# Sample attention of a hybrid encoder layer: keys turned by VectorE in 32x32 squares, FoX scores as plain fp32 products, only the wanted output blocks turned

## The reference, cut to what matters

```
# FoX branch, 8 heads x 64: 512 cached keys and the 16 new ones
s = q @ k_all.T / 8 + c[q] - c[k]      (masked where k > q)
o_fox = softmax(s) @ v_all
# memory branch, 4 heads x 128: 256 cached keys
o_mem = softmax(qm @ mk.T / sqrt(128)) @ mv
```

## Time and profile before

| | before |
|---|---|
| timed runs | 1926.58 to 1926.63 us, median 1926.61 |
| span of the profiled execution | 1926.4 us |
| PE busy | 1903.4 us, 99% |
| DVE, ACT, POOL busy | 1222.8, 842.7, 516.6 us |
| DMA, mean | 105 GB/s |
| FoX samples on PE | about 545 to 668 us |
| memory samples on PE | about 780 to 864 us |

### The profile page before, as it was taken

The page is one execution under the profiler, slowest core; times in us unless marked ns, Lnnn a source line. Parts: engine busy times, 40 slices in busy tenths (PEclk is TensorE's granted clock), DMA queues, the critical chain, the costliest instruction groups (busy, mean ns, idle before and its releaser), DMA issues. The chain is left out here.

```text
span 1926.4 us, 33099 instructions
## 1 busy us (share of the span) xinstructions
PE 1903.4 (99%) x12655; PEld 1869.4 (97%) x12655; DVE 1222.8 (63%) x2293; ACT 842.7 (44%) x1672; POOL 516.6 (27%) x547
## 2 busy tenths in 40 slices
PE   9999999999999999999999999999999999999998
PEld 8999999999999999999999999999999999999997
DVE  6685545454557666554334467687777977777765
ACT  7454434353546544443223332344444544444445
POOL 1004324250612123000000004276544433333320
PEclk9999999999999999999999999999999999999999
DMA  6451312213266643444233222233333433333323
GB/s 197 114 134 50 94 47 66 83 35 94 55 231 206 203 137 99 146 154 131 64 104 93 70 88 72 94 100 91 122 89 92 123 91 88 88 88 88 89 93 99
DMA packets 243601, 202.40 MB, mean 105 GB/s; under 512 B 16750, under 2 KB 217966, under 8 KB 243317
## 3 DMA queue, kind: packets, MB, share of 16 engines
q1 hardware_dynamic: 243445, 200.29, 34.8%
HBM read 166.62 MB, written 33.64 MB: 104 GB/s over the span
## 5 line engine op out<-in xcount | busy, mean ns | idle before, releaser
L1654 PE MATMUL ps<-act_hi,w_hi 128*128 128x384 f32 x1128 | 386.9, 343 | 0.9 <-DVE w_lo L597 0.6
L1654 PE MATMUL ps<-act_hi,w_lo 128*128 128x384 f32 x1128 | 378.0, 335 | 0.0
L1654 PE MATMUL ps<-act_lo,w_hi 128*128 128x384 f32 x1128 | 377.6, 335 | 0.0
L597 DVE TENSOR_TENSOR w_lo<-w_raw,w_hi 128x512 fp32r<-128x512 f32 (+1 forms) x200 | 198.0, 990 | 122.3 <-ACT w_hi L579 121.7
L1638 PE MATMUL ps<-ffs_hi,w_hi 128*128 128x288 f32 x832 | 245.8, 295 | 1.0 <-DVE h L2646 0.6
L1638 PE MATMUL ps<-ffs_hi,w_lo 128*128 128x288 f32 x832 | 245.2, 295 | 0.0
L1638 PE MATMUL ps<-ffs_lo,w_hi 128*128 128x288 f32 x832 | 244.9, 294 | 0.0
L1623 PE MATMUL ps<-bp_hi,pw_hi 128*128 128x288 f32 x784 | 231.6, 295 | 0.2 <-DVE pw_lo L2601 0.2
L1623 PE MATMUL ps<-bp_lo,pw_hi 128*128 128x288 f32 x784 | 231.3, 295 | 0.0
L1623 PE MATMUL ps<-bp_hi,pw_lo 128*128 128x288 f32 x784 | 231.2, 295 | 0.0
L579 ACT ACTIVATE w_hi<-w_raw 128x512 fp32r<-128x512 f32 (+1 forms) x200 | 152.6, 763 | 164.5 <-PE ps L1638 119.4
(11 more groups left out here) (356 smaller groups left out, 4190.7 us busy)
## 6 DMA issues: line engine op xcount, KB each, us to landing
w_raw<-in_w_down_dram SPq DMA_DIRECT2D x112, 256.0 KB, 3.4
pair_raw<-in_w_up_dram SPq DMA_DIRECT2D x28, 1024.0 KB, 5.5
w_raw<-in_w_in_dram SPq DMA_DIRECT2D x44, 512.0 KB, 4.4
merged<-prod SPq DMA_DIRECT2D x48, 192.0 KB, 2.0
prev<-merged SPq DMA_DIRECT2D x48, 192.0 KB, 3.8
foxs_vraw<-in_cache_fox_v_dram SPq DMA_DIRECT2D x8, 1024.0 KB, 6.1
foxs_kraw<-in_cache_fox_k_dram SPq DMA_DIRECT2D x7, 1024.0 KB, 5.6
x_in<-in_x_prompt_dram SPq DMA_DIRECT2D x8, 512.0 KB, 4.5
```

The source lines that it names most:

```text
L597: nc.vector.tensor_tensor(W[c % 2][1][:, 0:kt, :], w_raw[c % 2][:, 0:kt, :], W[c % 2][0][:, 0:kt, :].bitcast(F32), ALU.subtract).then_inc( ...
L1654: last = nc.tensor.matmul(bank(b)[:, 0:width], W[k][a][:, t, :], moving[z][:, t, j * width:(j + 1) * width], start=(t == 0 and n == 0), st ...
```

## The change

- Keys are loaded in another layout: four DMAs for each sample, one for each quarter y of the partitions, with rows of 512 bytes. Partition 32y + r gets tokens r, 32 + r and so on, and of them the 128 channels of group y.
- `turn_keys` is gone from PE. DVE turns the keys with its own transpose, which turns each 32x32 square in its place (`keys_turned`, four instructions a sample). Because of the new layout the squares make whole rows of keys, but the channels of a group now lie in another order (32 channels of each of four groups), and the queries (`qs_raw`, `mqs_raw`) are laid out in the same way. A mask `own_head`, made once by POOL, multiplies the queries so that other heads' rows are zero.
- FoX scores take the turned keys and the queries as they are, as plain fp32: 8 products of 128x264 in place of 24 fp32r ones, and no split. `kt` and `qpad` have two homes each, used in turn. Memory keys are turned into `kt_raw` and then split by ACT and DVE as before, from SBUF.
- The values' result is read by ACT (not DVE) in four small copies, of each head's rows only the columns wanted (`own_values`), into an `om` of 128x128. One transpose turns it. `out_sum` of FoX has four small additions in place of two.
- In the projection of q and k, ACT copies the sample tokens in four quarters in place of one, and DVE's rest of them is gone (8 blocks each).

```diff
+        qs_raw = tensor("qs_raw", [P, BT, P], R3_AT + 7168)
+        ks_raw = tensor("ks_raw", [P, BT, P], R3_AT + 11264)
...
+        sf = dict(kraw=tensor("foxs_kraw", [P, PAST // QUAD, P], R_AT), kt=[tensor(f"foxs_kt{k}", [P, 4, ST * P + NQ], R_AT + 8192 + 16 * (ST * P + NQ) * k) for k in range(2)],
+                  qpad=[tensor(f"foxs_qpad{k}", [P, 4 * P], R_AT + 25088 + 2048 * k) for k in range(2)],
...
+                  kt=parts("mems_kt", [P, 4, MT * P], R_AT + 8192), kt_raw=tensor("mems_kt_raw", [P, 4, MT * P], R_AT + 8192 + 16 * MT * P), v=parts("mems_v", [P, MT, 512], R_AT + 16384),
...
+        def out_turned():
+            return ps[:, 1, 384:512].rearrange("p (h x q) -> p h x q", x=2, q=NQ)
...
+        def own_values(a, h):
+            r = slice(2 * NQ * h, 2 * NQ * (h + 1))
+            w = 2 * P if a.new else 4 * P
+            cs = slice(h * FD, (h + 1) * FD) if a.new else slice(h * MD, (h + 1) * MD)
+            return r, ps[r, 4, :].rearrange("p (g w) -> p g w", w=w)[:, :, cs]
+
+        def p_stationary(a, t, g):
+            return a.b["pt"][:, t, g, :, :, :].rearrange("p h x q -> p (h x q)")
...
+        heads_by_squares = lambda c: c.rearrange("l b (t r) h d -> (l b) r t (h d)", r=QUAD)
+        samples = [Samples(sf, True, ST, FH, [qs_raw], 0, heads_by_squares(cache_fox_k), heads_flat(cache_fox_v)),
+                   Samples(sm, False, MT, MH, MQS, NB, heads_by_squares(cache_mem_k), heads_flat(cache_mem_v))]
...
+            def send_keys(a, i):
+                for y in range(4):
+                    sp.dma_start(raw_keys(a, i)[quadrant(y), :, :], a.kd[i][:, :, y * P:(y + 1) * P]).then_inc(sa["k_in"], 16)
...
+            pool.wait_ge(at_s["masked"], MASKS * BT)
+            then_mask(nc.gpsimd.memset(own_head[:], 1.0))
+            then_mask(nc.gpsimd.affine_select(out=own_head[:], in_=own_head[:], compare_op=ALU.is_ge, fill=0.0, base=0,
+                                              pattern=[[-QUAD, 4], [0, NQ]], channel_multiplier=1))
+            then_mask(nc.gpsimd.affine_select(out=own_head[:], in_=own_head[:], compare_op=ALU.is_ge, fill=0.0,
+                                              base=QUAD - 1, pattern=[[QUAD, 4], [0, NQ]], channel_multiplier=-1))
...
+                nc.gpsimd.tensor_copy(sf["kt"][i % 2][:, :, ST * P:ST * P + NQ],
+                                      ks_raw[:, :, i * NQ:(i + 1) * NQ]).then_inc(sa["k_new"], 1)
...
-            def turn_keys(a, i, part):
-                c = a.base + i
-                if part == 0:
-                    pe.wait_ge(sa["k_in"], 16 * (c + 1))
-                    if i == 0 and a.new:
-                        pe.wait_ge(at_s["s_read"], UNITS)
-                    elif i == 0:
-                        pe.wait_ge(at_s["exp"], UNITS + M_UNITS)
-                for j in (2 * part, 2 * part + 1):
-                    if 4 * c + j >= 2:
-                        pe.wait_ge(sa["kt_lo"], 4 * c + j - 1)
-                    raw = raw_keys(a, i)
-                    for t in range(a.tiles):
-                        last = nc.tensor.transpose(ps[:, j % 2, t * P:(t + 1) * P], raw[:, t, j * P:(j + 1) * P], ident[:])
-                    last.then_inc(sa["kt_over"], 1)
...
+                    for j in range(4):
+                        if a.new:
+                            pe.wait_ge(sa["kt_over"], 4 * c + j + 1)
+                            for z in range(parts_of):
+                                last = nc.tensor.matmul(ps[:, 2 + z, 0:w], b["qpad"][i % 2][:, j * P:(j + 1) * P],
+                                                        b["kt"][i % 2][:, j, z * w:(z + 1) * w], start=(j == 0), stop=(j == 3))
+                        else:
+                            pe.wait_ge(sa["kt_lo"], 4 * i + j + 1)
+                            for y in range(2):
+                                last = nc.tensor.matmul(ps[:, 2, 0:w], b["qpad"][0][:, j * P:(j + 1) * P], b["kt"][y][:, j, :],
+                                                        start=(j == 0 and y == 0), stop=(j == 3 and y == 1))
...
                 def turned_out():
                     pe.wait_ge(sa["om"], c)
-                    if i < NB:
-                        pe.wait_ge(sa["s_read" if a.new else "exp"], c + 1)
-
-                    for j in range(4):
-                        lo = j * P - (j % 2 * 2 * NQ if a.new else j * NQ)
-                        last = nc.tensor.transpose(ps[:, 2, lo:lo + P], b["om"][:, j * P:(j + 1) * P], ident[:])
-                    last.then_inc(sa["ot_over"], 1)
+                    if i >= 2:
+                        pe.wait_ge(sa["o_done"], c - 1)
+                    nc.tensor.transpose(ps[:, 1, 384:512], b["om"][:], ident[:]).then_inc(sa["ot_over"], 1)
...
+                if part == 0 and i:
+                    act.wait_ge(sa["pv_over"], c)
+                    if c >= 2:
+                        act.wait_ge(sa["ot_over"], c - 1)
+                    for h in range(4):
+                        r, own = own_values(a, h)
+                        last = nc.scalar.activation(b["om"][r, :].rearrange("p (g w) -> p g w", g=2 if a.new else 1), own,
+                                                    ACT.Copy)
+                    last.then_inc(sa["om"], 1)
...
-                        last = nc.scalar.activation(rest[0][:, s.i, :], src[:, LAST:TB], ACT.Copy, scale=scale)
+                        for y in range(4):
+                            last = nc.scalar.activation(rest[quadrant(s.i), y, :], src[quadrant(y), LAST:TB],
+                                                        ACT.Copy, scale=scale)
...
+            def keys_turned(a, i, part):
                 c = a.base + i
+                if part == 0:
+                    dve.wait_ge(sa["k_in"], 64 * (c + 1))
+                    if i >= 2 and a.new:
+                        dve.wait_ge(sa["s_over"], c - 1)
+                    elif i and not a.new:
+                        dve.wait_ge(sa["s_over"], c)
                 for j in (2 * part, 2 * part + 1):
-                    dve.wait_ge(sa["kt_hi"], 4 * c + j + 1)
-                    nc.vector.tensor_tensor(a.b["kt"][1][:, j, 0:a.tiles * P], ps[:, j % 2, 0:a.tiles * P],
-                                            a.b["kt"][0][:, j, 0:a.tiles * P].bitcast(F32),
-                                            ALU.subtract).then_inc(sa["kt_lo"], 1)
+                    nc.vector.transpose((sf["kt"][i % 2] if a.new else sm["kt_raw"])[:, j, 0:a.tiles * P],
+                                        raw_keys(a, i)[:, :, quadrant(j)]).then_inc(sa["kt_over"], 1)
...
+                if i >= 2 and a.new:
+                    dve.wait_ge(sa["s_over"], c - 1)
...
+                    if a.new:
+                        pad = sf["qpad"][i % 2][:, 2 * x * P:2 * (x + 1) * P].rearrange("p (m y w) -> p m y w", m=2, y=4)
+                        pad = pad[:, :, :, x * NQ:(x + 1) * NQ]
+                        new, n = qs_raw[:, 2 * x:2 * x + 2, i * NQ:(i + 1) * NQ], 2
+                    else:
+                        pad = sm["qpad"][0][:].rearrange("p (j z y q) -> p j z y q", j=4, z=2, q=NQ)[:, :, x, :, :]
+                        new, n = MQS[x][:, :, i * NQ:(i + 1) * NQ].bitcast(F32), 4
+                    last = nc.vector.tensor_tensor(pad, new.unsqueeze(2).broadcast_to([P, n, 4, NQ]),
+                                                   own_head[:].unsqueeze(1).broadcast_to([P, n, 4, NQ]), ALU.mult)
                 last.then_inc(sa["q_pad"], 1)
+
+            def keys_lo(a, i, part):
+                if a.new:
+                    return
+                for j in (2 * part, 2 * part + 1):
+                    dve.wait_ge(sa["kt_hi"], 4 * i + j + 1)
+                    nc.vector.tensor_tensor(sm["kt"][1][:, j, :], sm["kt_raw"][:, j, :], sm["kt"][0][:, j, :].bitcast(F32),
+                                            ALU.subtract).then_inc(sa["kt_lo"], 1)
...
+                    reached(dve, "head_mask", 3)
                     queries(a, 0)
...
+                        for r, y, hs, js in out_places():
+                            last = nc.vector.tensor_tensor(o_part[y, js, :], out_turned()[r, hs, 0, :], b["o_low"][r, hs, :], ALU.add)
...
-                if part == 0 and i:
-                    masked_out()
...
                 elif part == 1:
+                    if i + 1 < NB:
+                        keys_turned(a, i + 1, 0)
+                        if not a.new:
+                            keys_turned(a, i + 1, 1)
                     dve.wait_ge(sa["pt_hi"], c + 1)
                     last = nc.vector.tensor_tensor(p_parts(a, 1), p_turned(a), p_parts(a, 0).bitcast(F32), ALU.subtract)
...
                 elif part == 2:
+                    if i + 1 < NB:
+                        if a.new:
+                            keys_turned(a, i + 1, 1)
+                        keys_lo(a, i + 1, 1)
                     if i and a.new and i + 1 < NB:
                         out_lo()
-                    if i + 1 < NB:
-                        keys_lo(a, i + 1, 1)
```

(27 more changed lines are left out.)

147 lines of the change are left out of this document (58 added, 89 removed).

## The result

The changed kernel takes 1940.64 us in the median of 4 runs (1938.24 to 1942.63), the kernel before 1926.62 (1926.58 to 1927.17 beside it). The ratio is 1.0070, with a 95% interval of 1.0058 to 1.0082: 14.0 us slower, where 9.6 us faster was forecast. The runs of the changed kernel now spread over 4 us. The profiled execution is the fastest of the four: it took 1938.24 us, and its span is 1936.3.

What follows compares the result with a forecast made beforehand. PE's list of work plus its few waits was taken as the bound. Terms -19.5 + 2.1 + 4.2 + 2.4 + 1.2 = -9.6 took 1926.6 to 1917 us, range 1908 to 1930.

Steps and rivals of the forecast that it cites:

- PE's own work: PE in the sample stages: 192 key transposes (-21.0) and 48 output transposes (-5.2) fewer, FoX scores +6.7; together -19.5 us.
- The mask: First FoX scores wait 3.0 us, not 0.4, for masked queries; the second sample's key wait goes; +2.1 us.
- ACT's copies: Memory samples: PE waits 0.6 us in 7 samples for ACT's four output copies behind p; +4.2 us.
- DVE's row: FoX part 1: where `w_lo` stands, queries come late and PE waits 0.8 us, three times; +2.4 us.
- The key landing: FoX keys: samples last at least landing (7 us) plus DVE's 5.1 us; wait 0.2 us in 6 samples, +1.2 us.
- keys at half rate: Rival: FoX key DMAs to 32 partitions land in 8.2 to 8.4 us; 1919 to 1920 us alone; chance 0.15.
- keys late everywhere: Rival: FoX keys land in 12 us in half the samples, 8.6 in the others; +15.3, 1931 us; chance 0.09.

Runs made afterwards that it cites:

- run 1: The changed kernel with POOL copying the new keys of sample i+1 ahead of its work on the new values of sample i; 1933.42 us, ratio 1.0027.
- run 3: (also `wide_keys`) The changed kernel with each sample's keys in four DMAs to all 128 partitions, rows of 512 bytes; 1934.31 us, ratio 1.0039.
- run 2: (also `whole_keys`) The changed kernel with each sample's keys in one DMA to 128 partitions, rows of 2 KB; 1930.08 us, ratio 1.0014.
- run 12: The `mended` kernel with each sample's keys in one DMA to 128 partitions; 1923.04 us, ratio 0.9978.
- `mended`: `both_orders` plus POOL's mask ahead of its wait for the output's store and ACT's memory output copies ahead of its exponent; 1929.88 us, ratio 1.0013.
- `two_queues`: The `mended` kernel with ACT issuing half of the key DMAs (partitions 64 to 127) of FoX samples 2 to 7; 1927.01 us, ratio 1.0003.
- `queries_first`: The changed kernel with DVE making the next FoX sample's queries first in part 1 and turning its keys last; 1938.92 us, ratio 1.0059.
- run 8: The changed kernel with 28 unused transposes on PE ahead of its wait for the first queries; one execution, 1934.1 us.
- `both_orders`: The changed kernel with POOL's order of run 1 and DVE's order of `queries_first` together; 1931.70 us, ratio 1.0022.

## Why the prediction was wrong

The measured 1940.6 us lies beyond the range and beyond every rival. The prediction had five terms, and one is missing. Against the traces:

- **PE's own work, -19.5: right.** 304 records fewer; the scores take 3.72 us (forecast 3.76), from the scaling of the only plain fp32 products by columns.
- **The mask, +2.1: right in its wait, wrong in its sum.** 3.04 us of wait, forecast 3.0. The scores behind it took 1.67 more at the low clock.
- **ACT's copies, +4.2: right.** 3.7 us; four copies take 1.11 us, forecast 1.06. Waits of 0.4 us for p and of 0.7 for queries came on top.
- **DVE's row, +2.4: too small.** The transposes are right (0.65 us, forecast 0.6). But `w_lo` starts 10.2 to 11.3 us after the scores (run 1), where I had worked out 8.6, so PE waits 1.5 us in three samples, not 0.8: 4.5.
- **The key landing, +1.2: the step that failed.** "A sample can't be shorter than landing + 5.1" counts one load, its own landing and one engine. In its place PE waited 13.1 us at four scores for POOL's copies of new keys, and lost clock behind three of these waits. The runs show four things that the step left out. A load to 32 partitions is slow (209 GB/s in the changed kernel against 300 in run 3 with the same bytes and rows), and 1 MB then takes 5.0 us in place of 3.5. Four issues hold SP for 1.9 to 3.4 us. The price is paid less by the keys than by what is under way beside and behind them: values, new values, bias. In sample 1 the bias landed at 572.2 in place of 569.7, and PE's wait for p grew from 0.3 to 1.97 us. And from the new values it went through POOL's queue, where the copy of new keys stands behind them.
- **How far the rate alone goes.** At full rate (run 2) the new values still land in 6.3 us, halfway between 5.3 and 7.3, and POOL's copies still hold up three scores. There the values' DMA is issued 2.4 us behind that of the keys; in the kernel before it is 3.9 to 4.7. SP sends keys once the last ones are turned, and that is now DVE's work, behind the queries: in run 2 the keys leave about 1.1 us after the scores start or could start, in the kernel before 0.7 to 1.9 us ahead of them. No run takes this part by itself. Changing POOL's order gave 7.2 us back (run 1), the full rate 10.6 (run 2); with both orders, mask and copies mended the full rate still gives 6.8 (run 12), so the two overlap only in part.
- **The clock: no term at all.** What the waits and the work leave of the 15.25 us is its cost. PE came into the stage 0.5 us earlier in the trace of the changed kernel. FoX's own share of PE's work, up to the last values, is -9.7; the waits grew from 2.1 to 19.7 us, +17.6; the rest is 15.25 + 0.5 + 9.7 - 17.6, some 7.8 us. The four slow groups of scores alone make 1.67 + 1.77 + 2.60 + 1.77 = 7.8; that leaves nothing for the projection products that ran slowly behind the wait for p, so the balance is good to a microsecond or two.

The rival "keys at half rate" had the right cause for a part of it. The Trainium skill, "SBUF — State Buffer", section "Door 1: The DMA port swizzle", gives 189 GB/s for 32 partitions and 328 for all of them at 1 MiB; the traces come near both, with 199 to 219 and, in rows of 512 bytes, 263 to 324. I priced the rate through the keys' own wait, at 3.3 us. The rival "keys late everywhere" had the right sign at 1931, but a place that the trace does not show: no score waited for turned keys in the changed kernel. What I should have asked is how long before the scores POOL's copies of the new keys end; the earlier trace rows shows one of them, at the one place where another wait hid it.

What stays open: with both orders and the full rate (run 12) the time is 1923, not 1917. Its waits (3.6 us for p in memory, 3.3 for turned keys, 2.2 for the memory branch's queries, 1.9 for p in FoX) are of that size, but I did not take them apart by runs.

## What to carry to other kernels

When PE's work between two meeting points gets shorter, list every engine that must arrive at the meeting point, with the slack that each has now, also those that cause no wait yet: here POOL had 0.6 us and lost it. When a DMA is split or reshaped, price it by the queue: its rate over its span of partitions, its issues, the moment at which it is sent, and every transfer beside and behind it. And price a wait of PE of about 3 us at its own length and, here, 1.5 to 3 us on top.

## What the runs showed of the hardware that was not expected

- Behind waits of 3.0 us and more before scores PE's clock mostly fell to 0.50, and the scores took 5.2 to 6.8 us in place of 3.7: 14 times of 17 over the traces with changed FoX samples. It is no sharp line: it fell behind 1.97 us in the changed kernel and 2.56 in `whole_keys`, and not behind 2.20, 2.55 (`mended`), 3.21 (`two_queues`), 3.30 (`queries_first`) and 3.31 (`wide_keys`, 3.83 us for the scores). With transposes of no use in the wait it stayed at 1.00 (run 8).
- POOL's copy of 128x64 took 1.08 to 1.18 us while DVE split values or weights (rests of 128x1024, both inputs in SBUF), and 0.24 to 0.32 otherwise. DVE's two multiplications took 1.29 us while POOL worked on the new values (1.57 in `whole_keys`), 0.50 otherwise.
- DVE turns 128x512 fp32 in 0.65 us and 128x256 in 0.35.
- The versions with the changed FoX samples spread by 3.7 to 8.1 us from run to run (`both_orders` 1928.0 to 1936.2), the kernel before by 3.5 us over 33 runs. What makes the spread is not shown.
